# Causal attention on one Trainium2 core: the mask added by VectorE in the bank, the rows scaled by GpSimd

## The chip, the cores and the metric

One NeuronCore of a Trainium2 (trn2) chip runs the whole program. The metric is the device time of one execution in microseconds (us); lower is better. Everything is float32.

## What is computed

One inference step of a two-layer decoder trunk for 512 prompt tokens and 64 sample tokens (8 sequences of 8). Each layer projects its input, runs three mixers (causal pooling, a gated linear recurrence, latent attention), merges them through gates and ends in a gated feed-forward part with a short convolution. The change lies in the attention of the prompt: 8 heads, 512 queries, 512 keys, causal.

```python
s = q_lat . ckv + q_pe . kpe                       # per head, queries x keys
s = where(q_pos >= k_pos, s * MLA_SCALE, -inf)
p = softmax(s, axis=-1)
o_lat = p . ckv                                    # then through w_uv, per head
```

## The kernel before, in words

The program is written engine by engine; each engine runs its instructions in the order of the text and waits on semaphores. A Python helper `signal(name, per_layer)` makes a semaphore that counts up by `per_layer` in each of the two layers, and `x.at(l, n)` means "n of them in layer l".

**The tiles.** The prompt's attention is cut into 64 score tiles, 32 a layer (`N_ATT`), of 128 queries each. Tile n belongs to head pair n // 8, query block i = n % 8 // 2 and head e = n % 2 of the pair. Since it is causal, block i has (i + 1) * 128 keys, so the eight tiles of a head pair have 128, 128, 256, 256, 384, 384, 512 and 512 keys. Four PSUM banks, four buffers `probs`, four `probs_t` and four sets of statistics rotate (`N_ATT_BUFS`).

**What each engine does for a tile.** TensorE computes the scores (L930) and adds the mask with a second matmul, identity times a 128x128 constant of 0 and -1e30, into the last 128 columns of the same bank (L931). VectorE takes the negated row maximum (L2035). ScalarE computes exp(score - max) into `probs` and the row sums with it (L1632). VectorE takes the reciprocal of the sum (L2043) and multiplies the row by it in place (L2045). TensorE transposes the tile in blocks of 128 (L939), ScalarE copies the blocks out of the bank into `probs_t` (L1623 called by `att_take`), and TensorE multiplies by the values once both heads of a block are there (L951). A float32 matmul stands in the trace as two records.

**The order, written out by hand.** TensorE's loop over n issues the scores of tile n+3, then the transposes of tile n, and after every odd n from 3 on the value product of the block before (L1520 to L1525). VectorE's loop (L2243 to L2249) does reciprocal and scaling of tile n, then the maximum of tile n+3; at n = 10, 18 and 26 it also copies the finished output of a head pair out of its bank (L2050). ScalarE's loop does the exponential of tile n, then the copy of tile n-2 (L1779 to L1787). The scores of tiles 0 to 2 are issued earlier, ahead of the last piece of an input projection (L1508). GpSimd does nothing in this stretch: its last instruction before it is one subtraction (L2810), its next one (`value_blocks`, L2817) waits until the sample attention behind it is done. After the 32 tiles comes the sample tokens' attention, on TensorE, VectorE and ScalarE, and after that the projections of the other mixers.

Of the kernel before, what the change touches and what calls it, by code (L numbers as in the profile page):

```python
# [20 lines left out]
ALU = mybir.AluOpType  # L21
# [4 lines left out]
P = 128  # L26
# [34 lines left out]
N_ATT_BUFS = 4  # L61
N_CHUNK = SEQ // CHUNK
# [114 lines left out]
N_ATT = MLA_HEADS * N_CHUNK  # L177
# [20 lines left out]
def build(nc, xT_in, w_stream, small_in, att_in, const_in, pages_in, kpe_in, page_table, pool_state,  # L198
          hgrn_state, conv_state, yT, ckv_out, kpe_out, pool_out, hgrn_p_out, hgrn_s_out, conv_out):
    with ExitStack() as ctx:  # L200
# [3 lines left out]
        def sem(name):  # L204
            return ctx.enter_context(nc.semaphore(name))
# [38 lines left out]
        q96 = q96_flat.rearrange("p (j e t) -> p j e t", j=N_PAIRS, e=2)  # L244
        q96_by_tile = q96_flat.rearrange("p (x a e t) -> p x a e t", x=2, a=2, e=2)
        k96 = k96_flat.rearrange("p (j e t) -> p j e t", j=N_PAIRS, e=2)
# [10 lines left out]
        probs = [r1[:, o + i * SEQ:o + (i + 1) * SEQ] for i in range(N_ATT_BUFS)]  # L257
# [127 lines left out]
        causal = const[:, C_CAUSAL:C_CAUSAL + P]  # L385
# [4 lines left out]
        ident = const[:, C_ID:C_ID + P]  # L390
# [9 lines left out]
        def att_stat(n, which):  # L400

            c = 4 * (n % N_ATT_BUFS) + which
            return stat[:, c:c + 1]
# [34 lines left out]
        def att_bank(n):  # L438

            return bank[(0, 1, 6, 5)[n % N_ATT_BUFS]]  # L440
# [26 lines left out]
        def signal(name, per_layer):  # L467
            return Signal(sem(name), per_layer)
# [51 lines left out]
        qpe_s_ready = signal("qpe_s_ready", 3)  # L520

        att_scores = signal("att_scores", N_ATT)
        att_max = signal("att_max", N_ATT)
        att_exp = signal("att_exp", N_ATT)
        att_recip = signal("att_recip", N_ATT)
        att_probs = signal("att_probs", N_ATT)
# [152 lines left out]
        def level_scaled(eng, h, first=0, end=len(LEVELS)):  # L679

            for half, out, t0, t1 in levels(h, first, end):
                _, hi, _ = parts(out, half)
                _, qhi, _ = parts(q_hg[:, h, t0:t1], half)
                ins = eng.tensor_tensor(hi, hi, qhi, ALU.mult)
            return ins
# [201 lines left out]
        def _(pe):  # L887
# [36 lines left out]
            def att_score(l, n):  # L924
                j, r = divmod(n, 2 * N_CHUNK)
                i, e = divmod(r, 2)
                if n >= N_ATT_BUFS:
                    pe.wait_ge(*att_exp.at(l, n - N_ATT_BUFS + 1))
                t0, keys = i * P, (i + 1) * P
                pe.matmul(att_bank(n)[:, 0:keys], q96[:, j, e, t0:t0 + P], k96[:, j, e, 0:keys], start=True, stop=False)  # L930
                pe.matmul(att_bank(n)[:, t0:keys], ident, causal, start=False, stop=True).then_inc(att_scores.sem, 1)  # L931

            def att_turn(l, n):
                i = n % (2 * N_CHUNK) // 2
# [497 lines left out]
            with pe.Fori(0, DEPTH) as l:  # L1432
# [13 lines left out]
                for j in range(4):  # L1446
                    n = 2 + j // 2
# [15 lines left out]
                for j in range(4):  # L1463
                    n = 4 + j // 2
# [19 lines left out]
                for j in range(N_PAIRS):  # L1484
                    pe.wait_ge(*taken_at(l, TILE_KN + j - 4))
                    pe.matmul(slot(TILE_KN + j)[:, 0:SEQ], w_uk[:, j * P:(j + 1) * P], ckv[:, 0:SEQ],
                              start=True, stop=True).then_inc(tile_ready.sem, 1)
# [9 lines left out]
                for m, part in [(m, part) for part in range(2) for m in range(4)] + [(4, 0), (4, 1)]:  # L1497
                    rows = min(P, T - m * P)
                    if part == 0:
                        pe.wait_ge(*taken_at(l, TILE_HI + m - 4))  # L1500
                    if m == 0:
                        pe.wait_ge(*w_ready[part].at(l, 16 * 4))
                    if (m, part) == (4, 0):
                        pe.wait_ge(*q_rope.at(l, 2))
                        pe.wait_ge(*k_rope.at(l, 4))
                        pe.wait_ge(*taken_at(l, TILE_QLS + 1))
                        pe.wait_ge(*taken_at(l, TILE_HI + 2))
                        for n in range(N_ATT_BUFS - 1):  # L1508
                            att_score(l, n)
                    both = 1 if m < 4 else 2  # L1510
                    for k in range(KD):
                        g = SAMPLES * (k % both)
                        mm = pe.matmul(slot(TILE_HI + m)[g:g + rows, part * 256:(part + 1) * 256],  # L1513
                                       xT[:, k, m * P:m * P + rows], w_slot[part][:, k * 256:(k + 1) * 256],
                                       start=(k < both), stop=(k >= KD - both))
                    if part == 1:
                        mm.then_inc(tile_ready.sem, 1)
                for tile in (TILE_HI + 3, TILE_HI + 4):
                    pe.wait_ge(*taken_at(l, tile))
                for n in range(N_ATT):  # L1520
                    if n + N_ATT_BUFS - 1 < N_ATT:
                        att_score(l, n + N_ATT_BUFS - 1)
                    att_turn(l, n)
                    if n % 2 and n >= 3:
                        att_values(l, n // 2 - 1)  # L1525
# [21 lines left out]
                n = N_LOADS_PROJ  # L1547
                for tile in range(TILE_U, TILE_YPOOL):
                    j = (tile - TILE_U) % 2
# [59 lines left out]
        def _(act):  # L1609
# [14 lines left out]

            def att_softmax(l, n):
                keys = (n % (2 * N_CHUNK) // 2 + 1) * P
                act.wait_ge(*att_max.at(l, n + 1))
                if n >= N_ATT_BUFS:

                    act.wait_ge(*att_turned.at(l, n - N_ATT_BUFS + 1))  # L1630
                    act.wait_ge(*att_recip.at(l, n - N_ATT_BUFS + 1))
                act.activation(probs[n % N_ATT_BUFS][:, 0:keys], att_bank(n)[:, 0:keys], ACT.Exp,  # L1632
                               bias=att_stat(n, 0), accum_out=att_stat(n, 2)).then_inc(att_exp.sem, 1)
# [70 lines left out]
            with act.Fori(0, DEPTH) as l:  # L1704
# [71 lines left out]
                for g in range(1, P // ROPE):  # L1776
                    copy(qpe_s[g * ROPE:(g + 1) * ROPE, :, :, :], qpe_s[0:ROPE, :, :, :]).then_inc(qpe_s_ready.sem, 1)

                att_softmax(l, 0)  # L1779
                for n in range(1, N_ATT + 2):  # L1780
                    if n < N_ATT:
                        att_softmax(l, n)
                    if n == 2:
                        act.wait_ge(*tile_ready.at(l, TILE_HI + 5))
                        copy(v_hg[0:SAMPLES, 4, :], slot(TILE_HI + 4)[SAMPLES:P, 0:512]).then_inc(hi_half_taken.sem, 1)
                    if n >= 2:
                        att_take(l, n - 2)  # L1787
# [199 lines left out]
        def _(dve):  # L1987
# [42 lines left out]
            def att_stats(l, n):  # L2030
                keys = (n % (2 * N_CHUNK) // 2 + 1) * P
                dve.wait_ge(*att_scores.at(l, n + 1))
                if n >= N_ATT_BUFS:
                    dve.wait_ge(*att_exp.at(l, n - N_ATT_BUFS + 1))
                dve.tensor_reduce(att_stat(n, 0), att_bank(n)[:, 0:keys], AX_X, ALU.max, negate=True  # L2035
                                  ).then_inc(att_max.sem, 1)

            def att_normalise(l, n):
                keys = (n % (2 * N_CHUNK) // 2 + 1) * P
                dve.wait_ge(*att_exp.at(l, n + 1))  # L2040
                if n >= N_ATT_BUFS:
                    dve.wait_ge(*att_probs.at(l, n - N_ATT_BUFS + 1))
                dve.reciprocal(att_stat(n, 3), att_stat(n, 2)).then_inc(att_recip.sem, 1)  # L2043
                dve.wait_ge(*att_recip.at(l, n + 1))
                dve.tensor_scalar(probs[n % N_ATT_BUFS][:, 0:keys], probs[n % N_ATT_BUFS][:, 0:keys], att_stat(n, 3), None,  # L2045
                                  ALU.mult).then_inc(att_probs.sem, 1)

            def take_head_pair(l, j):
                dve.wait_ge(*att_pv.at(l, N_CHUNK * (j + 1)))
                dve.tensor_copy(o_mla[:, j, 0:SEQ], pv_bank(j)).then_inc(att_out_taken.sem, 1)  # L2050
# [84 lines left out]
            with dve.Fori(0, DEPTH) as l:  # L2135
# [105 lines left out]
                        dve.tensor_copy(v_hg[0:rows, m, :], slot(TILE_HI + m)[0:rows, 0:512]).then_inc(tile_dve.sem, 1)  # L2241

                for n in range(N_ATT):  # L2243
                    att_normalise(l, n)
                    if n + N_ATT_BUFS - 1 < N_ATT:
                        att_stats(l, n + N_ATT_BUFS - 1)

                    if n >= 10 and n % (2 * N_CHUNK) == 2:
                        take_head_pair(l, n // (2 * N_CHUNK) - 1)  # L2249
# [65 lines left out]
                for i, g in enumerate(GROUP_OF):  # L2315
# [12 lines left out]
                    e = ext[:, g, :]  # L2328
# [331 lines left out]
        def _(pool):  # L2660
# [14 lines left out]
            def ends_scaled(l, h):  # L2675
                pool.wait_ge(*ends_exp.at(l, h + 1))
                pool.tensor_tensor(decayed[:, h % 2, 0, :], decayed[:, h % 2, 0, :], q_hg[:, h, :], ALU.mult
                                   ).then_inc(lev_ready.sem, 1)

            def value_blocks(l, h):  # L2680

                pool.tensor_tensor(v_blocks,  # L2682
                                   v_hg[0:SAMPLES, 4, h * P:(h + 1) * P].unsqueeze(1).broadcast_to(
                                       [SAMPLES, S_PAIRS, P]),
                                   own_rows.unsqueeze(2).broadcast_to([SAMPLES, S_PAIRS, P]), ALU.mult
                                   ).then_inc(blocks_ready.sem, 1)
# [119 lines left out]
            with pool.Fori(0, DEPTH) as l:  # L2806

                pool.wait_ge(*prep_dve.at(l, 8))
                pool.wait_ge(*q_rope.at(l, 2))
                pool.tensor_tensor(log_k, log_k, logf, ALU.subtract).then_inc(log_k_ready.sem, 1)  # L2810

                pool.wait_ge(*smp_new_rows.at(l, 2))
                pool.wait_ge(*smp_cols_taken.at(l, S_PAIRS))
# [72 lines left out]
                for q in range(N_QUADS):  # L2886
# [12 lines left out]
                    if q >= HK:  # L2899
                        for x in range(2):  # L2900
                            j = 2 * (q % HK) + x
# [231 lines left out]
```

## Time and profile before

| | |
|---|---|
| median of 3 runs | 2267.76 us |
| lowest, highest | 2265.02, 2270.11 us |
| the profiled execution's own time | 2267.23 us |
| its span, first to last instruction | 2265.4 us |
| mean granted TensorE clock | 0.994 |
| busy: TensorE matmul / weight loads | 2196.5 / 1691.6 us |
| busy: VectorE / ScalarE / GpSimd | 1183.0 / 526.5 / 993.9 us |
| prompt attention, layer 1 | about 151 to 209 us |
| prompt attention, layer 2 | ends about 1333 us |

The page calls TensorE PE (PEld for its weight loads), VectorE DVE, ScalarE ACT, GpSimd POOL and SyncE SP. Busy time is per engine; a time in the chain of waits is the stretch for which an instruction was the last thing the end of the program waited for. L931 is line 931 of the kernel.

### The profile page before, as it was taken

How to read it: one execution, taken by the hardware profiler on the slowest of the kernel's cores; microseconds unless marked ns; L12 is line 12 of the kernel's file. 1: busy time of each engine (PE TensorE's matmuls, PEld its weight loads, DVE VectorE, ACT ScalarE, POOL GpSimd, SP SyncE). 2: the span in 40 equal slices, each digit the busy share in tenths (PEclk: the TensorE clock that was granted, in tenths of full speed). 3: DMA queues.
4: the chain of work that ended last, by engine and by line, in shares of the span. 5: the costliest groups of instructions: out<-in, count | busy, mean ns of one | idle time of the engine just before them, and what ended most of it. 6: DMA issues, size and time to landing. Idle time of an engine off the chain costs nothing.

```text
span 2265.4 us, 36978 instructions
## 1 busy us (share of the span) xinstructions
PE 2196.5 (97%) x11856; PEld 1691.6 (75%) x11856; DVE 1183.0 (52%) x2124; ACT 526.5 (23%) x1112; POOL 993.9 (44%) x1128
## 2 busy tenths in 40 slices
PE   8999999999999999999899999999999999999996
PEld 6775777777777777777676757777777777777775
DVE  0545666333578666661216346753335776666523
ACT  1434343111132001100134343531111311001002
POOL 0000046667665666633300000465666566666251
PEclk9999999999999999999999999999999999999998
DMA  5322113222132222222132221131221322222211
GB/s 210 101 84 66 43 63 114 84 75 77 55 126 75 74 76 88 71 72 77 38 133 86 75 67 42 63 133 66 84 84 57 120 80 74 74 74 70 96 52 42
DMA packets 51616, 183.54 MB, mean 81 GB/s; under 512 B 7234, under 2 KB 27970, under 8 KB 37762
## 3 DMA queue, kind: packets, MB, share of 16 engines
q1 hardware_dynamic: 50882, 178.49, 22.9%
q10 hardware_dynamic: 576, 3.06, 0.3%
q8 instruction: 84, 1.38, 0.2%
q14 instruction: 74, 0.61, 0.1%
HBM read 172.35 MB, written 9.18 MB: 80 GB/s over the span
## 4 chain that ended last, share of the span: by engine, by line
PE 91%; DVE 3%; issue 2%; POOL 1%; ACT 1%; SPq 1%; DMA 0%; DVEq 0%; ACTq 0%
PE ps L1219 25%; PE ps L1139 22%; PE ps L1261 16%; PE ps L898 12%; PE ps L1513 3%; PE ps L930 1%; PE ps L1427 1%; PE ps L1291 1%; PE ps L951 1%; PE ps L939 1%; PE ps L919 1%; PE ps L1079 1%; PE ps L983 1%; PE ps L1413 1%; PE ps L1057 1%
## 5 line engine op out<-in xcount | busy, mean ns | idle before, releaser
L1219 PE MATMUL ps<-lq,mreg 128*128 128x288 f32 x1008 | 251.3, 406 | 0.0
L898 PE MATMUL ps<-xT,wring 128*128 128x288 f32 (+2 forms) x960 | 236.5, 408 | 2.7 <-DVE o_mla L2289 1.4
L1219 PEld LDWEIGHTS ps<-lq,mreg 128*128 128x128 f32 x1008 | 191.5, 190 | 52.9
L1623 ACT ACTIVATE r<-ps 128x288 f32<-128x288 f32 (+7 forms) x264 | 112.8, 431 | 480.1 <-PE ps L1139 257.0
L898 PEld LDWEIGHTS ps<-xT,wring 128*128 128x128 f32 x960 | 183.2, 191 | 54.4 <-issue 2.2
L1219 PE MATMUL ps<-xT,wring 128*128 128x288 f32 x672 | 169.8, 406 | 0.0
L1219 PEld LDWEIGHTS ps<-xT,wring 128*128 128x128 f32 x672 | 127.7, 190 | 35.3
L1139 PE MATMUL ps<-r,kbuf 128*128 128x288 f32 x576 | 143.6, 406 | 0.0
L1139 PEld LDWEIGHTS ps<-r,kbuf 128*128 128x128 f32 x576 | 109.4, 190 | 30.2
L1952 ACT ACTIVATE r<-r 128x592 f32<-128x592 f32 x44 | 30.7, 697 | 428.5 <-DVE r L2594 428.5
L2783 POOL TENSOR_TENSOR kbuf<-o_mla 128x288 f32<-128x288 f32 x42 | 33.3, 792 | 207.8 <-DVE o_mla L2558 207.8
L1623 ACT ACTIVATE o_mla<-ps 128x288 f32<-128x288 f32 (+1 forms) x108 | 45.2, 420 | 326.2 <-PE ps L1261 214.5
L2810 POOL TENSOR_TENSOR kbuf<-kbuf,lq 128x2304 f32<-128x2304 f32 x2 | 10.1, 5054 | 248.4 <-DVE side L2221 248.4
L2682 POOL TENSOR_TENSOR mreg<-vbuf,const 64x512 f32<-64x512 f32 x8 | 8.3, 1032 | 251.8 <-PE ps L1541 243.1
L2594 DVE SCALAR_TENSOR_TENSOR r<-r,small 128x592 f32<-128x592 f32 x88 | 106.4, 1209 | 12.4 <-DVE r L2591 12.0
L2591 DVE SCALAR_TENSOR_TENSOR r<-r,small 128x592 f32<-128x592 f32 x88 | 104.5, 1188 | 12.4 <-DVE r L2588 9.7
L1139 PE MATMUL ps<-xT,wring 128*128 128x288 f32 x384 | 97.0, 406 | 0.0
L1261 PE MATMUL ps<-r,side 128*128 128x288 f32 x372 | 92.7, 407 | 0.8 <-DVE r L2605 0.8
L1219 PE MATMUL ps<-lq,wring 128*128 128x288 f32 x336 | 88.3, 406 | 0.0
L1219 PE MATMUL ps<-xT,mreg 128*128 128x288 f32 x336 | 88.3, 406 | 0.0
L1139 PEld LDWEIGHTS ps<-xT,wring 128*128 128x128 f32 x384 | 73.0, 190 | 20.2
L1139 PE MATMUL ps<-lq,r 128*128 128x288 f32 x336 | 87.4, 406 | 0.0
(435 smaller groups left out, 4540.6 us busy)
## 6 DMA issues: line engine op xcount, KB each, us to landing
wring<-w_stream SPq DMA_DIRECT2D x100, 1024.0 KB, 4.9
side<-w_stream SPq DMA_DIRECT2D x18, 704.0 KB, 4.5
r<-pages_in SPq DMA_DIRECT2D x80, 128.0 KB, 2.2
vbuf<-w_stream SPq DMA_DIRECT2D x12, 512.0 KB, 3.7
r<-w_stream SPq DMA_DIRECT2D x12, 512.0 KB, 3.6
wring<-w_stream SPq DMA_DIRECT2D x8, 704.0 KB, 4.1
r<-w_stream SPq DMA_DIRECT2D x6, 704.0 KB, 4.1
mreg<-pages_in SPq DMA_DIRECT2D x32, 128.0 KB, 2.1
```

The source lines that it names most:

```text
L898: mm = pe.matmul(out[0:w.shape[-1], a * 512:a * 512 + hi - lo], w, x[:, lo:hi], start=(k == 0), stop=(k == len(pairs) - 1))
L919: mm = pe.matmul(slot(tile + j)[:, a * 512:a * 512 + hi - lo], w, xT[:, k, lo:hi], start=(k == 0), stop=(k == KD - 1))
L930: pe.matmul(att_bank(n)[:, 0:keys], q96[:, j, e, t0:t0 + P], k96[:, j, e, 0:keys], start=True, stop=False)
L1139: mm = pe.matmul(banks[name], ws[:, k * P:(k + 1) * P], xs[:, k, :], start=(k == 0), stop=(k == n - 1))
L1219: mm = pe.matmul(up_sum[name], ws[:, k * P:(k + 1) * P], xs[:, k, :], start=(k == 0), stop=(k == HK - 1))
L1261: mm = pe.matmul(res_bank(which, m, i - 1), ws[:, k * P:(k + 1) * P], x, start=(k == 0), stop=(k == len(xs) - 1))
L1513: mm = pe.matmul(slot(TILE_HI + m)[g:g + rows, part * 256:(part + 1) * 256], xT[:, k, m * P:m * P + rows], w_slot[part][:, k * 256:(k + 1) ...
L1623: return act.activation(out, in_, func, **more)
L1952: act.activation(conv_h[u][0][:, 0:CX - 2], conv_h[u][0][:, 0:CX - 2], ACT.Silu).then_inc(silu_done.sem, 1)
L2591: dve.scalar_tensor_tensor(out=out, in0=src[:, 1:CX - 1], scalar=scalar(col + 2 * KF), in1=out, op0=ALU.mult, op1=ALU.add).then_inc(conv_s ...
L2594: dve.scalar_tensor_tensor(out=out, in0=src[:, 2:CX], scalar=scalar(col + 4 * KF), in1=out, op0=ALU.mult, op1=ALU.add).then_inc(conv_done. ...
L2783: pool.tensor_tensor(up_v[u], up_u2[u], up_p5s[u], ALU.add).then_inc(up_v_ready.sem, 1)
```

## The change

The causal matmul leaves TensorE: the score matmul now both starts and stops the bank. VectorE adds the 128x128 constant to the last 128 columns of the bank, waits for its own addition, and takes the maximum; the semaphore `att_max` now counts two a tile. The multiplication by the reciprocal leaves VectorE; its reciprocal alone stays there. GpSimd waits for the reciprocal and multiplies the row, the statistic broadcast along the row, for the 32 tiles of a layer in one loop behind its L2810.

```diff
-        att_max = signal("att_max", N_ATT)
+        att_max = signal("att_max", 2 * N_ATT)
...
-                pe.matmul(att_bank(n)[:, 0:keys], q96[:, j, e, t0:t0 + P], k96[:, j, e, 0:keys], start=True, stop=False)
-                pe.matmul(att_bank(n)[:, t0:keys], ident, causal, start=False, stop=True).then_inc(att_scores.sem, 1)
+                pe.matmul(att_bank(n)[:, 0:keys], q96[:, j, e, t0:t0 + P], k96[:, j, e, 0:keys], start=True, stop=True
+                          ).then_inc(att_scores.sem, 1)
...
             def att_softmax(l, n):
-                act.wait_ge(*att_max.at(l, n + 1))
+                act.wait_ge(*att_max.at(l, 2 * n + 2))
...
             def att_stats(l, n):
                 dve.wait_ge(*att_scores.at(l, n + 1))
                 if n >= N_ATT_BUFS:
                     dve.wait_ge(*att_exp.at(l, n - N_ATT_BUFS + 1))
+                diagonal = att_bank(n)[:, keys - P:keys]
+                dve.tensor_tensor(diagonal, diagonal, causal, ALU.add).then_inc(att_max.sem, 1)
+                dve.wait_ge(*att_max.at(l, 2 * n + 1))
                 dve.tensor_reduce(att_stat(n, 0), att_bank(n)[:, 0:keys], AX_X, ALU.max, negate=True
                                   ).then_inc(att_max.sem, 1)
...
-            def att_normalise(l, n):
+            def att_reciprocal(l, n):
                 dve.wait_ge(*att_exp.at(l, n + 1))
                 if n >= N_ATT_BUFS:
                     dve.wait_ge(*att_probs.at(l, n - N_ATT_BUFS + 1))
                 dve.reciprocal(att_stat(n, 3), att_stat(n, 2)).then_inc(att_recip.sem, 1)
-                dve.wait_ge(*att_recip.at(l, n + 1))
-                dve.tensor_scalar(probs[n % N_ATT_BUFS][:, 0:keys], probs[n % N_ATT_BUFS][:, 0:keys], att_stat(n, 3), None,
-                                  ALU.mult).then_inc(att_probs.sem, 1)
...
                 for n in range(N_ATT):
-                    att_normalise(l, n)
+                    att_reciprocal(l, n)
                     if n + N_ATT_BUFS - 1 < N_ATT:
                         att_stats(l, n + N_ATT_BUFS - 1)
...
+            def att_normalise(l, n):
+                keys = (n % (2 * N_CHUNK) // 2 + 1) * P
+                pool.wait_ge(*att_recip.at(l, n + 1))
+                row = probs[n % N_ATT_BUFS][:, 0:keys]
+                pool.tensor_tensor(row, row, att_stat(n, 3).broadcast_to([P, keys]), ALU.mult).then_inc(att_probs.sem, 1)
...
                 pool.tensor_tensor(log_k, log_k, logf, ALU.subtract).then_inc(log_k_ready.sem, 1)
+                for n in range(N_ATT):
+                    att_normalise(l, n)
                 pool.wait_ge(*smp_new_rows.at(l, 2))
```

## Rows read from the trace of the kernel before

**Rows 1.** The page: busy times; the chain that ended last, by engine.

```profile
PE 2196.5 (97%) x11856; PEld 1691.6 (75%) x11856; DVE 1183.0 (52%) x2124; ACT 526.5 (23%) x1112; POOL 993.9 (44%) x1128
...
PE 91%; DVE 3%; issue 2%; POOL 1%; ACT 1%; SPq 1%; DMA 0%; DVEq 0%; ACTq 0%
```

**Rows 2.** Stretches: length, then each engine's busy us, granted clock, DMA share, GB/s.

```profile
176.60:190.10 13.50, 12.56 (x94) 9.08 (x93) 8.00 (x26) 7.80 (x24) 0.00 (x0) 1.00 0.53 157
236.00:246.00 10.00, 7.33 (x101) 5.68 (x101) 3.12 (x6) 3.10 (x9) 0.35 (x1) 1.00 0.10 27
1360.00:1370.00 10.00, 7.33 (x101) 5.68 (x101) 3.18 (x6) 3.16 (x9) 0.29 (x1) 1.00 0.10 27
1370.00:1375.00 5.00, 5.00 (x15) 4.13 (x16) 4.61 (x21) 0.00 (x0) 0.74 (x1) 0.66 0.00 0
```

**Rows 3.** Chain of waits, head pair 2 of layer 1: start us, us, what.

```profile
184.70 0.11 PE ps L939
...
185.67 0.26 PE ps L939
...
187.80 0.23 PE ps L931 x2
...
189.73 0.44 PE ps L939 x2
...
191.59 0.23 PE ps L931 x2
...
192.46 0.16 DVE stat L2043
...
193.12 0.55 PE ps L939 x3
...
194.90 0.44 PE ps L939 x4
...
195.99 0.54 PE ps L939 x4
...
198.19 0.11 PE ps L939
```

**Rows 4.** VectorE's groups by shape: count, busy us, mean ns, idle before.

```profile
L2035 DVE TENSOR_REDUCE stat<-ps 128x1 f32<-128x512 f32 x16 | 11.0, 689 | 8.6 <-PE ps L931 8.6
...
L2372 DVE TENSOR_TENSOR mreg<-ps,const 128x128 f32<-128x128 f32 x32 | 9.3, 292 | 1.1
...
L2050 DVE COPY o_mla<-ps 128x512 f32<-128x512 f32 x8 | 5.4, 680 | 0.0
...
L2035 DVE TENSOR_REDUCE stat<-ps 128x1 f32<-128x128 f32 x16 | 4.6, 288 | 6.5 <-PE ps L931 6.5
```

**Rows 5.** GpSimd's groups by shape, columns as in rows 4.

```profile
L2754 POOL TENSOR_TENSOR mreg<-wring 128x512 f32<-128x512 f32 x42 | 73.7, 1756 | 0.0
...
L2844 POOL TENSOR_TENSOR kbuf<-kbuf,wring 128x512 f32<-128x512 f32 x24 | 30.4, 1268 | 3.6 <-POOL kbuf L2840 3.2 <-PE ps L1139 0.3
...
L2797 POOL TENSOR_TENSOR r<-o_mla 128x64 f32<-128x64 f32 x42 | 13.8, 329 | 0.0
...
L675 POOL TENSOR_TENSOR r<-lq 128x256 f32<-128x256 f32 x14 | 9.0, 643 | 81.9 <-DVE r L2339 81.9
...
L2682 POOL TENSOR_TENSOR mreg<-vbuf,const 64x512 f32<-64x512 f32 x8 | 8.3, 1032 | 251.8 <-PE ps L1541 243.1 <-PE ps L1124 8.8
```

**Rows 6.** Timeline where GpSimd waited for VectorE: start us, us, what.

```profile
414.74 0.45 DVE L2463 TENSOR_TENSOR r<-r,ps 128x288 f32<-128x288 f32 x1 [3.27 <-PE ps L1139]
...
415.28 0.79 POOL L2870 TENSOR_TENSOR r<-r 128x288 f32<-128x288 f32 x1 [4.79 <-DVE r L2463]
```

**Rows 7.** Chain of waits at the layer's edges of the attention, columns as in rows 3.

```profile
153.13 0.22 PE ps L931 x2
...
206.62 0.55 PE ps L939 x3
...
207.75 1.03 PE ps L939 x8
```

More of the change, by code:

```diff
@@ L2034, in att_stats @@
                     dve.wait_ge(*att_exp.at(l, n - N_ATT_BUFS + 1))
+                diagonal = att_bank(n)[:, keys - P:keys]
+                dve.tensor_tensor(diagonal, diagonal, causal, ALU.add).then_inc(att_max.sem, 1)
+                dve.wait_ge(*att_max.at(l, 2 * n + 1))
                 dve.tensor_reduce(att_stat(n, 0), att_bank(n)[:, 0:keys], AX_X, ALU.max, negate=True
                                   ).then_inc(att_max.sem, 1)
-            def att_normalise(l, n):
-                keys = (n % (2 * N_CHUNK) // 2 + 1) * P
+            def att_reciprocal(l, n):
                 dve.wait_ge(*att_exp.at(l, n + 1))
```

## The prediction

> **What bounds the kernel now.** First the page's busy times and its chain [rows 1]: TensorE is busy for 97% of the span and makes 91% of the chain, so every us taken off or put on its path counts fully, and no other engine's total matters. Then the stretches: within one head pair of the prompt's attention, TensorE is busy 12.56 of 13.50 us, VectorE 8.00, ScalarE 7.80, GpSimd not at all [rows 2]. Last the chain through that pair [rows 3], which shows where the missing us goes. Read the starts of the transposes, two to a block: tile 16 at 184.70, 17 at 185.67, 18 at the end of the mask, 187.80 + 0.23 = 188.03, 19 at 189.73, 20 at 191.59 + 0.23 = 191.82, 21 at 193.12, 22 at 194.90, 23 at 195.99, 24 at 198.19. So the gaps inside a block (first head to second) are 0.97, 1.70, 1.30, 1.09, in sum 5.06 us, and the gaps between blocks 2.36, 2.09, 1.78, 2.20, in sum 8.43, together 13.49. Between blocks TensorE has transposes, a value product and scores to do; inside a block only one tile's transposes and one tile's scores, and there VectorE enters the chain.
>
> **The recurrence.** VectorE's reciprocal of tile n stands behind its maximum of tile n+2, which waits for the scores of n+2. Between these scores and the transposes of n, TensorE does the transposes of n-1, after an odd n-1 a value product, and the scores of n+3. So transposes n start at the later of two times: TensorE's own work done, or scores n+2 done + L, where L is maximum(n+2), reciprocal(n), scaling(n) and their hand-overs. Today, tile 21: scores 23 end at 191.82, the maximum begins 0.04 later, the reciprocal at 192.46, the transposes at 193.12, so L = 1.30 [rows 3]. The other waits have slack: exp(n) needs only maximum(n), two tiles earlier.
>
> **Part 1, the mask leaves TensorE.** 64 masks at 0.22 to 0.23 us [rows 3, 7], 14 us of TensorE's time in both layers. Where TensorE's own work ends last, the gain is real; where L ends last, scores end earlier and the chain behind them grows.
>
> **Part 2, the addition enters L.** VectorE's nearest row is 128x128 out of a bank with a constant, 0.29 us [rows 4]; writing back to the bank is not in it. With 0.04 for its own semaphore: 0.33. Bounds: 0.21 (the part of a duration that a following instruction does not see is 0.08, from 0.69 for the 512-wide maximum against 0.61 between its start and the reciprocal's [rows 3, 4]) and 0.44.
>
> **Part 3, the scaling moves to GpSimd.** Its two-input rows: 64 wide 0.33, 256 wide 0.64, 512 wide 1.27, and 1.76 for a 512-wide one beside VectorE's work on SBUF tensors [rows 5]. On the line 0.18 + 2.12 ns an element: 0.46, 0.72, 0.99, 1.26 us for 128 to 512 keys. The one with broadcast operands, 64 partitions and 512 wide, takes 1.03 [rows 5], which is the lower bound (0.39, 0.60, 0.82, 1.03); 1.76 in proportion is the upper. I take the line, since nothing says which of that row's two differences made it quicker. Hand-overs: VectorE to GpSimd 0.09 (415.19 to 415.28 [rows 6]), GpSimd to TensorE 0.08, half of the 0.16 that a dependent GpSimd instruction waits (3.2 us over the 20 such [rows 5]).
> The Trainium skill (Perfetto Trace Analysis, GPSIMD Engine Instruction) holds that a GpSimd span in a profile is unreliable and should be timed from start to start. By that the price could be off either way; my two bounds cover it, and the sum stays on the rows.
>
> **The new L.** 0.04 + 0.33 + maximum(n+2) + reciprocal 0.16 + 0.09 + GpSimd(n) + 0.08, the maximum at 0.21, 0.34, 0.48 or 0.61 for 128 to 512 keys (its duration less 0.08; the two ends [rows 4] and the line between). For the second heads of blocks 0 to 3:
> - block 0: 0.34 and 0.46, L = 1.50
> - block 1: 0.48 and 0.72, and the head-pair copy stands in between, 0.68 [rows 4] less 0.09: L = 2.49
> - block 2: 0.61 and 0.99, L = 2.30
> - block 3: 0.21 and 1.26, L = 2.17
>
> TensorE's own work in these four gaps is 0.75, 1.07, 0.55 and 0.87 (today's gap less the mask, and in blocks 1 and 2 less the waits of 0.41 and 0.53), so L decides all four: 8.46 against 5.06, **+3.40 a pair**. Between blocks TensorE's own work still ends last (block 1 to 2: L counted from scores 22 is 2.30 plus at most 0.5 because VectorE is still at tile 19, against 1.42 + 1.87 = 3.29): four masks less, **-0.90**. A transpose group after a pause costs about 0.1 more (0.55 for three at 193.12, 0.44 for four at 194.90, with 0.10 due to the value product behind [rows 3]); that is new in blocks 0 and 3: **+0.2**. A full head pair: **+2.7 us**.
>
> **The edges.** The three early scores save three masks, 0.66, on the path [rows 7]; tile 3's mask, 0.22. In the first pair there is no value product at first and no copy: block 0 +0.4, the next two gaps about 0, then +0.2, block 2 +0.6, then -0.2, block 3 +1.1, then -0.2 and 0.1 for the pause: with the start +1.1. The two middle pairs 5.4. The last pair: blocks 0 and 1 +0.53 and +0.79, two gaps between -0.45, +0.1; then no scores are left and **GpSimd alone ends last**: from scores 31 it needs 0.04 + 0.33 + 0.61 + 0.16 + 0.09 + 0.99 + 1.26 + 1.26 + 0.16 = 4.90 to transposes 31, where today it is 206.62 - 1.30 = 205.32 to 207.75 + 0.5 = 208.25, 2.93 [rows 7]: +1.97. Last pair +2.9. A layer: 1.1 + 5.4 + 2.9 = 9.4; both: **+18.8 us**.
>
> **What costs nothing.** VectorE: addition in (0.29), scaling out (0.29 to 0.49), its total falls or stays and it has idle time. GpSimd: 28 us more a layer in a stretch in which it had nothing; its next instruction waits for the end of the sample attention, so it delays nobody. SyncE's page loads start at half of the scores and have over 20 us. What follows the attention is TensorE's own chain, so the delay passes through. 2267.23 + 18.8 = **2286 us**; the profiled execution is 0.5 us below the median of the runs, which I neglect.
>
> **Rivals.**
> 1. *As above, chance 0.73.* With the broadcast row's price each pair is 0.59 cheaper and the tail 0.6: -4.8 in all, 2281. With 0.15 instead of 0.04 between addition and maximum, +3.
> 2. *GpSimd is slowed by VectorE, 2297, chance 0.10.* The row of 1.76 against 1.27 [rows 5] shows that it happens here. At that ratio 0.18, 0.29, 0.40 and 0.51 more for the four widths: 1.4 a pair, 11 in all. Against it: VectorE's work in this stretch reads banks and at most one SBUF tensor, the mask. The Trainium skill (GPSIMD Engine Reference, Key points) puts such contention on VectorE instructions in a 2-port mode or with two SBUF inputs, of which this stretch would have none; by that rule this rival falls.
> 3. *TensorE's clock falls, 2300, chance 0.08.* After a stretch 73% busy the granted clock over 5 us was 0.66, a part of them at 1.2 instead of 2.4 GHz, 1.7 us lost; after the same stretch in layer 1 it stayed at 1.00 [rows 2]. In the new attention TensorE would be some 10.7 of 16.2 us busy, 66%, in pauses of up to 1.7 us. One fall per head pair costs 8 x 1.7 = 14. The Trainium skill (TensorE: Matmul & The Clock Gate, A second HAM failure mode) tells of a kernel with such short pauses whose clock went back and forth. Against it: every pause is short, while before the fall there were several together.
> 4. *Faster, 2253, chance 0.05.* VectorE reaches reciprocal(n) before it matters, L hides behind TensorE's work, and the 64 masks come off: -14. It decides from L below 0.55 to 1.07 us inside a block. Against it: L is 1.30 today, and even a GpSimd as quick as VectorE would leave L at 1.3 to 2.1 with the addition in it.
> 5. *No change, chance 0.04.* The pieces cancel: each L would have to be 0.7 us shorter than computed.
>
> **The numbers.** The range takes rival 1 with the cheap GpSimd, some uncertainty of the edges and of the runs (2276), and reaches over rival 2 (2299). A difference of 0.2%, 4.5 us, is about what a measurement of this kernel tells from none. Faster is rival 4, 0.05; same is rival 5, 0.04; slower the rest, 0.91.
>
> **What the profile of the changed kernel would show.** No mask records on L931's place; an addition of about 0.3 us before each maximum; GpSimd's rows 0.46 to 1.26 us. In the chain, every second head of a block would have VectorE's addition, maximum, reciprocal and GpSimd's scaling before its transposes, with gaps of 1.5, 2.5, 2.3, 2.2, and gaps between blocks 0.2 shorter; a head pair takes 16.2 instead of 13.5 us. At the layer's last two tiles, GpSimd back to back. The prediction is wrong if GpSimd's rows lie outside 0.39 to 1.8, if the gaps inside a block are under 1.1 us, if the granted clock falls there, or if the attention's delay is made up before the layer ends.

## The result, and the profile after

| | before | after |
|---|---|---|
| median of the runs | 2268.51 us | 2282.17 us |
| lowest, highest | 2265.02, 2270.11 us | 2280.57, 2282.26 us |
| span of the profiled execution | 2265.4 us | 2280.4 us |
| mean granted TensorE clock | 0.994 | 0.991 |

The ratio of the times is 1.0061, with a 95% interval from 1.0048 to 1.0073: the changed kernel is 13.7 us slower. (A fourth run moved the median of before from 2267.76 to 2268.51.) Forecast were 2286, slower, and 2276 to 2299.

The page of the changed kernel, busy times and the chain by engine, beside [rows 1]:

```profile
PE 2190.2 (96%) x11728; PEld 1676.4 (74%) x11728; DVE 1171.5 (51%) x2124; ACT 527.4 (23%) x1112; POOL 1039.8 (46%) x1192
...
PE 81%; issue 10%; DVE 3%; POOL 3%; ACT 1%; SPq 1%; DMA 1%; DVEq 0%; POOLq 0%; ACTq 0%
```

TensorE has 128 records fewer, two for each of 64 masks, and yet the program is longer. The chain has lost some of TensorE's share to "issue": in the attention it now runs from one GpSimd instruction to the next and names nothing in between, so it can't be read there. The timeline can. Here are the stretches of the changed kernel, columns as in [rows 2]: one head pair's length in layer 1 (it reaches from the last transposes of pair 1 to the last of pair 2; [rows 2] has its pair cut at another point of the same round), then three stretches that we come back to.

```profile
187.11:202.55 15.44, 10.96 (x76) 6.68 (x76) 7.20 (x25) 7.89 (x24) 5.68 (x10) 1.00 0.29 84
...
160.00:165.00 5.00, 4.43 (x14) 1.95 (x13) 2.67 (x10) 2.65 (x9) 1.62 (x3) 0.66 0.82 346
...
213.00:220.00 7.00, 5.41 (x37) 3.96 (x39) 0.86 (x4) 2.90 (x6) 2.82 (x3) 0.76 0.18 47
...
246.00:262.00 16.00, 13.33 (x119) 10.48 (x114) 8.84 (x32) 3.09 (x8) 1.03 (x1) 0.89 0.05 16
```

A head pair takes 15.44 us where it took 13.50 [rows 2], and TensorE is busy for 10.96 of them, 1.6 less than before: it waits for 4.5 us, where it waited for 0.9.

The timeline of the changed kernel over that pair (start us, us, engine, what; in brackets the idle time before and what ended it), the transposes and, in block 1, all that lies in front of them:

```profile
189.11 0.27 PE L939 MATMUL ps<-const,r 128*128 128x128 f32 x1
...
190.67 0.33 PE L939 MATMUL ps<-const,r 128*128 128x128 f32 x1 [0.64 <-POOL r L2684]
...
192.70 0.38 PE L939 MATMUL ps<-const,r 128*128 128x128 f32 x2
192.90 0.30 DVE L2036 TENSOR_TENSOR ps<-ps,const 128x128 f32<-128x128 f32 x1 [1.87 <-PE ps L930]
...
193.24 0.56 DVE L2038 TENSOR_REDUCE stat<-ps 128x1 f32<-128x384 f32 x1
193.71 0.68 DVE L2049 COPY o_mla<-ps 128x512 f32<-128x512 f32 x1
...
194.31 0.15 DVE L2045 RECIPROCAL stat<-stat 128x1 f32<-128x1 f32 x1
...
194.54 0.61 POOL L2684 TENSOR_TENSOR r<-r,stat 128x256 f32<-128x256 f32 x1 [2.81 <-DVE stat L2045]
...
195.21 0.44 PE L939 MATMUL ps<-const,r 128*128 128x128 f32 x2 [1.26 <-POOL r L2684]
...
196.91 0.49 PE L939 MATMUL ps<-const,r 128*128 128x128 f32 x3
...
199.16 0.55 PE L939 MATMUL ps<-const,r 128*128 128x128 f32 x3 [1.54 <-POOL r L2684]
...
200.55 0.60 PE L939 MATMUL ps<-const,r 128*128 128x128 f32 x4
...
202.62 0.66 PE L939 MATMUL ps<-const,r 128*128 128x128 f32 x4 [1.03 <-POOL r L2684]
...
204.54 0.27 PE L939 MATMUL ps<-const,r 128*128 128x128 f32 x1
```

Every second head's transposes, at 190.67, 195.21, 199.16 and 202.62, were released by GpSimd's L2684; every first head's did not wait. In block 1 the whole of L stands there in order: addition at 192.90, maximum 0.34 later, the copy of a head pair, the reciprocal, GpSimd 0.23 after the reciprocal began, the transposes 0.06 after GpSimd ended. The gaps inside a block are 1.56, 2.51, 2.25 and 2.07 us, those between blocks 2.03, 1.70, 1.39 and 1.92. One thing to know for a comparison: a record of transposes that did not wait begins some 0.2 us before the scores in front of it are done, so these gaps inside a block are up to 0.2 longer, and those between blocks shorter, than starts taken from a chain as in [rows 3]. Taken from the timeline, like these, before has 1.08, 1.87, 1.47, 1.14 inside (5.6 in sum) and 2.25, 1.92, 1.61, 2.15 between (7.9). The change made it 8.4 and 7.0: **+2.8 inside, -0.9 between.**

GpSimd's groups in the attention of layer 1, changed kernel, columns as in [rows 5]:

```profile
L2684 POOL TENSOR_TENSOR r<-r,stat 128x512 f32<-128x512 f32 x7 | 7.3, 1039 | 4.3 <-DVE stat L2045 4.3
L2684 POOL TENSOR_TENSOR r<-r,stat 128x384 f32<-128x384 f32 x8 | 6.6, 826 | 9.2 <-DVE stat L2045 9.2
L2684 POOL TENSOR_TENSOR r<-r,stat 128x256 f32<-128x256 f32 x8 | 4.9, 613 | 12.2 <-DVE stat L2045 12.2
L2684 POOL TENSOR_TENSOR r<-r,stat 128x128 f32<-128x128 f32 x8 | 3.2, 399 | 43.1 <-DVE stat L2045 43.1
```

0.40, 0.61, 0.83 and 1.04 us: the lower bound of the forecast (0.39, 0.60, 0.82, 1.03), not its value (0.46, 0.72, 0.99, 1.26).

The end of layer 1's attention in the changed kernel's timeline, beside [rows 7]: with no scores left, three scalings stand in a row on GpSimd and TensorE waits for them.

```profile
213.71 2.82 POOL L2684 TENSOR_TENSOR r<-r,stat 128x384 f32<-128x384 f32 x3 [1.92 <-DVE stat L2045]
...
214.59 0.55 PE L939 MATMUL ps<-const,r 128*128 128x128 f32 x3 [1.76 <-POOL r L2684]
...
216.07 1.97 PE L939 MATMUL ps<-const,r 128*128 128x128 f32 x8
```

Where the 15.0 us between the two profiled spans came from, read at the same instructions of both traces: 1.0 during the first weight loads, before any changed instruction runs; -0.9 a layer ahead of transposes 0; from transposes 0 to transposes 31, 57.7 against 49.0 us in layer 1 and 56.5 against 49.0 in layer 2; and about -0.5 in what lies behind.

### The profile page after: what moved, and what is told of

Read it like the earlier page. It is cut to its first block, busy times and chain, and to the rows that moved or that the text cites. A ratio compares the mean times of both kernels' runs of the same rounds, so it can differ in the third digit from the quotient of the medians.

```text
span 2280.4 us, 36974 instructions
## 1 busy us (share of the span) xinstructions
PE 2190.2 (96%) x11728; PEld 1676.4 (74%) x11728; DVE 1171.5 (51%) x2124; ACT 527.4 (23%) x1112; POOL 1039.8 (46%) x1192
## 4 chain that ended last, share of the span: by engine, by line
PE 81%; issue 10%; DVE 3%; POOL 3%; ACT 1%; SPq 1%; DMA 1%; DVEq 0%; POOLq 0%; ACTq 0%
PE ps L1219 25%; PE ps L1139 21%; PE ps L1261 16%; PE ps L898 8%; POOL r L2684 2%; PE ps L1427 1%; PE ps L1291 1%; PE ps L1079 1%; PE ps L919 1%; PE ps L983 1%; PE ps L1057 1%; PE ps L1413 1%; PE ps L1025 1%; DMA wring<-w_stream 1%; POOL kbuf L2816 0%
## 5 line engine op out<-in xcount | busy, mean ns | idle before, releaser
L898 PE MATMUL ps<-xT,wring 128*128 128x288 f32 (+2 forms) x960 | 238.2, 411 | 3.0 <-DMA wring<-w_stream 1.5
L898 PEld LDWEIGHTS ps<-xT,wring 128*128 128x128 f32 x960 | 184.4, 192 | 55.2 <-issue 2.2
L2593 DVE SCALAR_TENSOR_TENSOR r<-r,small 128x592 f32<-128x592 f32 x88 | 106.3, 1208 | 12.4 <-DVE r L2590 12.1
L2590 DVE SCALAR_TENSOR_TENSOR r<-r,small 128x592 f32<-128x592 f32 x88 | 104.5, 1188 | 12.4 <-DVE r L2587 10.6
L2684 POOL TENSOR_TENSOR r<-r,stat 128x128 f32<-128x128 f32 (+3 forms) x64 | 45.4, 719 | 136.7 <-DVE stat L2045 136.7
```

What stands on the lines that cost most here:

```text
L898: mm = pe.matmul(out[0:w.shape[-1], a * 512:a * 512 + hi - lo], w, x[:, lo:hi], start=(k == 0), stop=(k == len(pairs) - 1))
L2590: dve.scalar_tensor_tensor(out=out, in0=src[:, 1:CX - 1], scalar=scalar(col + 2 * KF), in1=out, op0=ALU.mult, op1=ALU.add).then_inc(conv_s ...
L2593: dve.scalar_tensor_tensor(out=out, in0=src[:, 2:CX], scalar=scalar(col + 4 * KF), in1=out, op0=ALU.mult, op1=ALU.add).then_inc(conv_done. ...
L2684: pool.tensor_tensor(row, row, att_stat(n, 3).broadcast_to([P, keys]), ALU.mult).then_inc(att_probs.sem, 1)
```

## The experiments

One head pair, number 2 of layer 2, from its first transposes to the next pair's, gaps read from the timeline as above; the time is set against the runs of the kernel before that were made with it.

| kernel | gaps inside | gaps between | pair, us | time, us | before, us | ratio (95%) |
|---|---|---|---|---|---|---|
| before | 5.57 | 7.94 | 13.50 | | 2268.51 | |
| changed | 8.39 | 7.04 | 15.43 | 2282.17 | 2268.51 | 1.0061 (1.0048 to 1.0073) |
| mask alone | 7.13 | 7.05 | 14.18 | 2268.90 | 2268.92 | 1.0002 (0.9992 to 1.0011) |
| scaling alone | 7.06 | 7.93 | 14.99 | 2279.16 | 2268.92 | 1.0045 (1.0027 to 1.0064) |
| before, reciprocal early | 4.14 | 7.71 | 11.85 | 2258.18 | 2268.92 | 0.9947 (0.9930 to 0.9963) |
| changed, reciprocal early | 3.46 | 7.40 | 10.86 | 2246.68 | 2268.92 | 0.9901 (0.9884 to 0.9917) |
| mask alone, reciprocal early | 3.62 | 7.08 | 10.70 | 2246.36 | 2269.56 | 0.9893 (0.9876 to 0.9909) |
| changed, copy later | 7.47 | 7.37 | 14.84 | 2278.06 | 2269.56 | 1.0035 (1.0023 to 1.0048) |
| row times itself | 8.40 | 7.05 | 15.45 | 2280.54 | 2269.56 | 1.0044 (1.0027 to 1.0061) |
| row times constants | 8.95 | 7.05 | 16.00 | 2289.99 | 2271.32 | 1.0082 (1.0052 to 1.0113) |
| row minus reciprocal | 8.40 | 7.05 | 15.44 | 2279.84 | 2271.32 | 1.0037 (1.0021 to 1.0053) |

**The theory** is that of the prediction: VectorE's reciprocal of tile n stands behind its work on tile n+2, so TensorE's transposes of n wait for scores(n+2) plus L, and whatever is added to L is paid inside each block. **Rivals**: TensorE's relief counts everywhere; the longer way over three engines costs by itself; contention; the clock.

### The mask alone

```diff
 # changed kernel, with the scaling back on VectorE behind its reciprocal
+                dve.wait_ge(*att_recip.at(l, n + 1))
+                dve.tensor_scalar(probs[n % N_ATT_BUFS][:, 0:keys], probs[n % N_ATT_BUFS][:, 0:keys], att_stat(n, 3), None,
+                                  ALU.mult).then_inc(att_probs.sem, 1)
...
-                for n in range(N_ATT):
-                    att_normalise(l, n)
```

> The kernel before with the mask's half of the change alone: addition by VectorE, scaling still on VectorE. Order theory (the reciprocal of tile n stands behind the maximum of tile n+2, and the addition's 0.33 us lies in front of it): gaps inside a block grow by 0.28, 0.33, 0.33 and 0.23 us, gaps between blocks shrink by 0.22 each; a head pair 13.8 instead of 13.5 us, the layer's start 0.9 earlier, in all +0.5 us: 2268 to 2270. Rival, that TensorE's relief counts everywhere: 64 masks of 0.22 come off, 2254.

Measured: no change, 2268.90 against 2268.92. The gaps between blocks shrank by 0.9 a pair, and those inside grew by 1.56, 0.4 more than computed: by 0.33 in each of the first three blocks, the addition's own price, and by 0.57 in the last. Where that block's extra 0.24 comes from is open. The stretch of pair 2 in layer 1 of this kernel (length, then TensorE, its loads, VectorE, ScalarE, GpSimd):

```profile
185.99:200.19 14.20, 10.97 (x78) 6.68 (x77) 10.31 (x33) 8.11 (x24) 0.00 (x0) 1.00 0.28 77
```

1.6 us less TensorE work in a longer stretch: the 14 us of masks bought nothing. The rival of 2254 falls.

### The scaling alone

```diff
 # changed kernel, with the mask back on TensorE
-                pe.matmul(..., start=True, stop=True).then_inc(att_scores.sem, 1)
+                pe.matmul(..., start=True, stop=False)
+                pe.matmul(att_bank(n)[:, t0:keys], ident, causal, start=False, stop=True).then_inc(att_scores.sem, 1)
...
-                dve.tensor_tensor(diagonal, diagonal, causal, ALU.add).then_inc(att_max.sem, 1)
-                dve.wait_ge(*att_max.at(l, 2 * n + 1))
```

> The kernel before with the other half alone: mask still on TensorE, scaling on GpSimd at the 0.40 to 1.04 us that the changed kernel's trace shows. Order theory: gaps inside a block 1.10, 2.04, 1.80 and 1.61 us (0.97, 1.70, 1.30, 1.09 before), gaps between blocks unchanged, a head pair 15.0 us, about 6 us a layer: 2280. Rival, that the two halves cost alike: 2275.

Measured 2279.16, +10.2, and 15.0 us a pair, as computed. The two halves alone give 0.0 and +10.2, together +13.7; the 3.5 us between sum and whole are within what the three intervals leave (about 2, 4 and 3 us either way). The scaling is what costs; the mask breaks even to within 2 us: its head pairs are 0.68 longer, and the start of each layer is 0.9 earlier.

### The reciprocal in front of the next tiles' maximum

```diff
                 for n in range(N_ATT):
                     att_normalise(l, n)           # att_reciprocal(l, n) in the changed kernel
-                    if n + N_ATT_BUFS - 1 < N_ATT:
-                        att_stats(l, n + N_ATT_BUFS - 1)
+                    if n >= 1 and n + N_ATT_BUFS - 2 < N_ATT:
+                        att_stats(l, n + N_ATT_BUFS - 2)
```

This is the run that decides about the theory: all the work, all the hand-overs stay, and only the place of the reciprocal in VectorE's queue changes. On the kernel before:

> The kernel before with VectorE's loop shifted by one: reciprocal and scaling of tile n now stand in front of the maximum of tile n+2. Order theory: the waits of 0.4 and 0.5 us in blocks 1 and 2 go with the pauses that follow them, a head pair 12.4 instead of 13.5 us: -8 us, 2260. Rival, that exp or the bank rotation holds the chain: 2267.

Measured 2258.18. The pair takes 11.85 us, less than the 12.4 expected: all four gaps inside a block fell, not only the two with a wait. Its pair 2 of layer 1: TensorE has no idle time left.

```profile
183.05:194.91 11.86, 11.86 (x95) 8.91 (x94) 8.26 (x25) 7.82 (x24) 0.00 (x0) 1.00 0.39 113
```

On the changed kernel:

> The changed kernel with VectorE's loop shifted by one: reciprocal(n) in front of addition and maximum of tile n+2. Order theory: addition, maximum and GpSimd's scaling lie beside two tiles of TensorE's work (2.6 us or more), L is hidden nearly everywhere, the 64 masks come off TensorE: a head pair 10.8 to 11.3 us, 2245 to 2252. Rival, that the longer path over three engines costs by itself (hand-overs, contention, clock falls): 2265 to 2280.

Measured 2246.68: from 0.6% slower to 1.0% faster by two lines. The timeline of this kernel around the second head of block 2:

```profile
184.73 0.15 DVE L2045 RECIPROCAL stat<-stat 128x1 f32<-128x1 f32 x1
...
184.97 0.83 POOL L2684 TENSOR_TENSOR r<-r,stat 128x384 f32<-128x384 f32 x1 [0.39 <-DVE stat L2045]
185.23 0.49 PE L939 MATMUL ps<-const,r 128*128 128x128 f32 x3
185.43 0.30 DVE L2036 TENSOR_TENSOR ps<-ps,const 128x128 f32<-128x128 f32 x1 [0.55 <-PE ps L930]
...
185.85 0.55 PE L939 MATMUL ps<-const,r 128*128 128x128 f32 x3
```

The reciprocal of the tile transposed at 185.85 was taken at 184.73, before the addition on the later tile, and GpSimd's 0.83 us lie beside TensorE's work. The gap is 0.62 us where it was 2.25. Hand-overs between three engines cost nothing when they are ahead of time; the rival falls.

Then the same order with the mask on VectorE and the scaling there too:

> VectorE's loop shifted by one and the mask added by VectorE, but the scaling still on VectorE; GpSimd idle as before. Order theory: L is hidden, but VectorE now has about 10.5 us of work a head pair (8 additions of 0.33, maxima 3.3, reciprocals 1.5, scalings 2.5, a copy 0.6) beside TensorE's 10.7, so it runs late now and then: a head pair 11.0 to 11.8 us, 2248 to 2256. It tells whether the scaling on GpSimd earns anything once the order is mended (2247 with it). Rival, that the mended order alone is all: 2247.

Measured 2246.36, and 10.70 us a pair: both below what was expected (2248 to 2256, 11.0 to 11.8), and the same time as with GpSimd. Its pair 2 of layer 1:

```profile
180.17:190.86 10.69, 10.65 (x77) 6.79 (x76) 9.93 (x33) 7.75 (x25) 0.00 (x0) 1.00 0.45 125
```

VectorE is busy 9.93 of 10.69 us and still in time, by 0.8 us a pair. So GpSimd earns nothing here: the mended order is worth 10.7 us (2258.18 against 2268.92), taking the masks off TensorE then another 12, near the 14 that 64 of them take, and the move to GpSimd 0, or a loss of about 1 (its pair is 0.16 longer, 10.86 against 10.70). These two kernels beat both that were compared.

### The copy of a head pair out of the way

```diff
-                    if n >= 10 and n % (2 * N_CHUNK) == 2:
+                    if n >= 11 and n % (2 * N_CHUNK) == 3:
                         take_head_pair(l, n // (2 * N_CHUNK) - 1)
```

> The changed kernel with the copy of a finished head pair moved on VectorE from behind the maximum of tile 8j+5 (in front of the reciprocal of 8j+3) to behind the next maximum, in front of a first head's reciprocal. Order theory: six gaps in block 1 of 2.5 us become 1.9, the gaps between blocks stay: -3.5 us, 2278.5. Rival, that the copy is hidden or only moves its cost: 2282.

Measured 2278.06, near the 2278.5 expected; against the kernel "row times itself" below, measured beside it and with the changed kernel's gaps, it is 2.5 us faster. The pair is 0.59 us shorter, near the copy's 0.68 in the timeline of the changed kernel, but not quite where expected: block 1's gap went from 2.51 to 1.91, the next one between blocks grew by 0.3, and block 2's fell by 0.3. Pair 2 of layer 1:

```profile
186.63:201.47 14.84, 11.18 (x77) 6.59 (x76) 7.30 (x25) 7.78 (x24) 5.68 (x8) 1.00 0.21 60
```

### GpSimd's price

The scalings took 0.83 to 0.87 of what the forecast took. Three kernels change only the operands or the operation of GpSimd's instruction, and so what the attention weights are.

```diff
-                pool.tensor_tensor(row, row, att_stat(n, 3).broadcast_to([P, keys]), ALU.mult)
+                pool.tensor_tensor(row, row, row, ALU.mult)                    # row times itself
+                pool.tensor_tensor(row, row, const[:, 0:keys], ALU.mult)       # row times constants
+                pool.tensor_tensor(row, row, att_stat(n, 3).broadcast_to([P, keys]), ALU.subtract)
```

> The changed kernel, but GpSimd multiplies the row by itself in place of the broadcast reciprocal (the attention weights are then squares of the exponentials, unscaled). If the broadcast operand is what made GpSimd's 512-wide rows 1.04 us where I had taken 1.26, they now take 0.46, 0.72, 0.99 and 1.26; the order theory then adds 0.06, 0.11, 0.16 and 0.23 to the gaps inside a block and 0.6 to the last tiles: +4.6 us on the changed kernel, 2287. If it was something else in this stretch, the rows stay as they are and so does the time, 2282.

GpSimd's 512-wide row in layer 1, the row times itself:

```profile
L2684 POOL TENSOR_TENSOR r<-r 128x512 f32<-128x512 f32 x8 | 8.3, 1041 | 4.3 <-DVE stat L2045 4.3
```

Not the broadcast by itself, then, and the time stays, 2280.54. A row times itself reads one tensor twice, so two different tensors and the operation were left to try.

> The changed kernel, but GpSimd multiplies the row by 128 to 512 columns of the table of constants in place of the reciprocal (the attention weights are not the softmax then): a product of two different tensors. What sets the width's price is open, since a row times itself took what a row times the broadcast statistic took. If it is that both inputs are read from the same few addresses, the 512-wide row now takes 1.26 us as the additions elsewhere do, and the kernel about 4.6 us more, 2286; if it is multiplication or the place in the program, it stays at 1.04 and 2281.

Measured 2289.99, 4 us above the 2286 expected, with the forecast's prices:

```profile
L2684 POOL TENSOR_TENSOR r<-r,const 128x512 f32<-128x512 f32 x6 | 7.6, 1270 | 3.7 <-DVE stat L2045 3.7
...
L2684 POOL TENSOR_TENSOR r<-r,const 128x128 f32<-128x128 f32 x8 | 3.7, 457 | 43.3 <-DVE stat L2045 43.3
```

> The changed kernel, but GpSimd subtracts the broadcast reciprocal from the row (weights not the softmax). If the operation sets the price (the rows of 1.27 are additions and subtractions), the 512-wide row takes 1.26 us and the kernel 2286; otherwise it stays at 1.04 and 2281.

Measured 2279.84, unchanged, and so are the rows:

```profile
L2684 POOL TENSOR_TENSOR r<-r,stat 128x512 f32<-128x512 f32 x8 | 8.3, 1039 | 4.3 <-DVE stat L2045 4.3
```

With two different full tensors the price is 0.46 to 1.27 us, the forecast's line; with one full tensor and a broadcast statistic, or the same one twice, 0.40 to 1.04, whether it multiplies or subtracts. And the kernel at the forecast's price is a test of the rest of the sum, by its trace: 16.0 us a pair, where 16.2 were forecast. Its time, 18.7 us over the kernel before where the sum had 18.8, agrees by luck: it comes from two runs, its interval reaches from 12 to 26 us, and it holds falls of TensorE's clock that the sum left out (granted 0.73 over 200 to 205 us and 0.50 over 220 to 225; pair 2 of layer 1 took 16.55 us, that of layer 2 16.00).

## Why the prediction was right

- **The recurrence held.** Second heads wait, first heads don't, in all four blocks and pairs; the order experiment shows the cause by taking it away.
- **Part 1**, masks: -0.9 a pair between blocks, as summed, and nothing inside them. The mask alone shows that the relief is eaten by the addition: no change in time, although 64 masks are gone from TensorE.
- **Part 2**, addition: 0.30 us by the trace and 0.34 from its start to the maximum's, 0.33 forecast. Write-back to the bank is no extra.
- **Part 3**, GpSimd: the mis-sized term. At 0.40 to 1.04 instead of 0.46 to 1.26, a pair costs 0.56 less (15.44 against 16.0 with two full tensors). Seven or so such pairs and the tail are the 4.8 us that rival 1 gave for this case. The 64-partition row of [rows 5] was quick through its broadcast operands, not its 64 partitions: 128 partitions with one broadcast input take the same. 2281 was the value to take; 2282 was measured. Two rows of [rows 5] spoke for it. Besides that one, the 256-wide row L675 has a broadcast second input too (by the kernel's text one column of each group, subtracted from a row of the same tensor), over all 128 partitions, and took 0.64 where the line gives 0.72: the prediction lists it among the rows behind its line, though it lies 0.08 under it. The line fits rows with two full tensors.
- **Hand-overs**: reciprocal's start to GpSimd's 0.23 (0.25 forecast), GpSimd's end to the transposes 0.05 to 0.06 (0.08).
- **The edges**: transposes 0 came 0.9 us earlier relative to the delay before them, as summed. The last pair's GpSimd queue is there; the tail cost about 1 us with the cheaper scalings. Layer 2, where the clock stayed at 1.00 through the attention's pairs, gives 56.5 - 49.0 = 7.5 us; at the forecast's price it was 59.0 - 49.0 = 10.0, the forecast 9.4 + 0.9 = 10.3.
- **Rival 2, contention**: did not occur. GpSimd's rows spread by a few ns around their means, beside VectorE's work on banks, with the constant mask as its one SBUF tensor of any width. The Trainium skill (GPSIMD Engine Reference, Key points) puts contention on VectorE instructions in a 2-port mode or with two SBUF inputs; the addition, the maximum, the copy and the reciprocal have at most one of them, and this trace agrees: no row above 1.04 us. In the changed kernel with the reciprocal early, where the scalings run beside additions, the 384-wide one takes 0.83 as well. No run here tests the case with two.
- **Rival 3, the clock**: occurred in part. By the prediction's own words a fall in the attention was a sign of its being wrong; it fell in two places of layer 1's, and they are worth 1.2 us of its 57.7. The changed kernel was granted 0.66 over 160 to 165 us, 0.76 over 213 to 220 and 0.89 over 246 to 262, where the kernel before had 1.00 in each: for parts of them TensorE ran at 1.2 instead of 2.4 GHz. Layer 1's first pair took 14.39 us where layer 2's took 13.62, which prices the first fall at 0.8; the second stands in the tail with about 0.4 up to transposes 31. The third lies behind the attention, where the projection L898 took 48.51 us instead of 46.82; these 1.7 us were given back in the recurrence stage, where TensorE waits for others (the delay between the two traces is 11.1 us at its start and 9.0 at its end). The mask-alone kernel had such falls as well (0.66 at 160 to 165, 0.89 at 246 to 262) and no change in time. And the falls don't follow from the pauses: "row minus reciprocal" has the changed kernel's gaps to 0.01 us and was granted 1.00 from 150 to 265 us, while "before, reciprocal early", whose pairs leave TensorE no idle time, was granted 0.66 over 215 to 220. The Trainium skill (TensorE: Matmul & The Clock Gate, A second HAM failure mode) tells of a kernel whose clock goes back and forth with short idle times between groups of matmuls; this trace does not show it: in six of the changed kernel's eight pairs the clock was 1.00 from end to end, while TensorE was busy 71% of the time (10.96 of 15.44).
- **Rivals 4 and 5** did not occur. Faster came only with the order changed.

How large the change's cost is in the end is less sure than the gaps. Of the 13.7 us, the interval leaves 10.9 to 16.6. The two kernels with the same gaps, "row times itself" and "row minus reciprocal", came out at +11.0 and +8.5, each against a kernel before that was slower in its round (2269.56 and 2271.32, against 2268.51). By the traces, without the clock, the change is worth 7.5 - 0.9 = 6.6 us a layer, 13.2 in all, where the sum with the cheap price has 14.0.

## What to carry to other kernels

Before moving work off the busiest engine, ask which queue the released time has to pass: work that stands behind a wait for a later tile is paid in full however idle its engine is, and moving one line up in that queue was worth 10.7 us here, and turned the change from +0.6% to -1.0%. Price a moved instruction by the row of its own kind (same operand pattern), even if it is the one with fewer partitions, before drawing a line through commoner rows.

## What the runs showed of the hardware

- GpSimd's tensor_tensor in float32 over 128 partitions: two different full inputs 0.46, 0.73, 1.00, 1.27 us for 128, 256, 384, 512 columns; one full input with a [128x1] broadcast, or one tensor as both inputs, 0.40, 0.61, 0.83, 1.04. Multiplication and subtraction cost the same. What in the engine makes the second input cheaper is open.
- VectorE's addition in place in a bank, 128x128: 0.30 us, the same as out of a bank into SBUF (0.29 [rows 4]).
- TensorE's granted clock fell in places of layer 1 where it had not before, and the places differ from kernel to kernel: at 160 to 165 us (0.66) in the changed kernel, the mask alone and row times constants, at 213 to 220 (0.76) in the changed kernel, the scaling alone, row times itself and "before, reciprocal early", and nowhere from 150 to 265 in row minus reciprocal, whose pauses are the changed kernel's. What ties them is open.
